# Two pieces of work change places on the tensor engine in the dilated attention scores

## The chip, the cores and the metric

One core of one Trainium2 chip runs the whole program. The metric is the device time of one execution in microseconds (us), the median of three. The engines are named as in the profile: PE is the tensor engine (PEld its weight loads, which overlap), DVE the vector engine, ACT the scalar engine, POOL GpSimd, SP the engine that issues most of the transfers. They run side by side, each through its own program in order, and wait for one another by semaphores: a number that one instruction raises when it is done, and that another waits for.

## The reference, cut to what matters

The program is a stack of layers over 512 tokens: two hybrid layers (delta rule and gated linear attention), then a stick-breaking attention, a feed-forward block, a dilated attention and another feed-forward block. The change is in the dilated attention alone, where the softmax of windowed scores is computed for three groups of eight heads each:

```python
DIL_GROUPS = ((128, 1), (512, 4), (2048, 16))
DIL_HEADS = 8
DIL_HEAD_DIM = 64
...
    s = jnp.einsum('brhnqd,brhnkd->brhnqk', q_blk, k_blk).astype(jnp.float32) * (dh ** -0.5)
    s = jnp.where(mask[None, None, None], s + bias[None, None, :, None], NEG)
    lse = jax.nn.logsumexp(s, axis=-1)
    p = jnp.exp(s - lse[..., None])
    o = jnp.einsum('brhnqk,brhnkd->brhnqd', p.astype(v_blk.dtype), v_blk)
```

All of it is in float32.

## The kernel before

`dilated_scores` does this in 15 **units**. A unit is a group g, a tile t of 128 query tokens, and either all eight heads against one tile of 128 keys (unit 0, and units 7 to 14, which are groups 1 and 2), or four heads against two tiles of keys (units 1 to 6, group 0). Either way a unit has 128 x 1024 scores. Its stages are:

- PE, `scores(n)` (line 2292): the products of queries and keys, with a contraction of 64 rows. They go to two of the four score banks in PSUM; even and odd units have two each.
- DVE, `bias(n)` (line 2343 twice, then 2346): adds the bias table while it copies the scores out to the SBUF tile `scores`, and takes the negated maximum of every row.
- ACT, `exps(n)` (line 2370): the exponentials in place, one instruction for each head, which also gives the row's sum.
- PE, `turn(n)` (line 2301): eight 128 x 128 transposes of the weights into PSUM banks 4 and 5.
- DVE, `turned(n)` (line 2354, twice): copies the turned weights to the SBUF tile `weights_turned`.
- PE, `values(n)` (line 2316): sixteen weight loads and matmul records (eight products of 64 columns), turned weights by values, into PSUM bank 6 or 7.
- ACT, `copy_out(n)` (line 2376): copies a finished tile of 512 columns to `numerators`, once for each of the 12 tiles.

`scores`, `weights_turned` and the score banks are double-buffered, by the parity of the unit. Banks 4 and 5 are not: `turn(n)` waits until the copies of unit n-1 are done. `scores(n)` waits until `bias(n-2)` is done, and `bias(n)` until unit n-2 is turned.

The order on each engine is written out by hand in one loop for each engine (the PE loop stands behind `values`, the DVE loop behind `turned`). PE runs `scores(n)`, `turn(n-1)`, `values(n-2)` for rising n; DVE `bias(n)`, `turned(n-1)`; ACT `exps(n)`, `copy_out(n-3)`. `dilated_merge` follows, whose first work on PE is at line 2405 and on ACT at line 2437; it begins when the stage's own work is done.

Of the kernel before, what the change touches and what calls it, by code (L numbers as in the profile page):

```python
# [127 lines left out]
def sbuf(nc, name, shape, dtype):  # L128
    NAMES[name] += 1
    return nc.sbuf_tensor(f"{name}_{NAMES[name]}", shape, dtype)  # L130


@contextmanager
def phase(nc, *names, landed=()):


    stack = ExitStack()
    NAMES["phase"] += 1
    sems = {n: stack.enter_context(nc.semaphore(f"{n}_{NAMES['phase']}")) for n in names}
    for s in USED:  # L140
        nc.sync.sem_clear(s)
    for held in HELD:
        held.close()
    yield named(**sems)
    HELD[:] = [stack]
    USED[:] = [*sems.values(), *landed]
# [2111 lines left out]
def dilated_scores(nc, k, q, kk, v, tables, num, top, total):  # L2258

    ps, con = k.ps, k.con
    ident = con[:, K_IDENT:K_IDENT + P]

    units = [(0, 0, 0, 8, 1)] + [(0, t, h0, 4, 2) for t in range(1, TT) for h0 in (0, 4)] \
        + [(g, t, 0, 8, 1) for g in (1, 2) for t in range(TT)]
    n_units = len(units)
    tiles = [n for n, (g, t, h0, heads, _) in enumerate(units) if h0 + heads == DIL_HEADS]
    with ExitStack() as stack, phase(nc, "scores", "half", "biased", "exp", "turned", "turned_read", "out", "out_copy") as s:  # L2270
        sc = stack.enter_context(sbuf(nc, "scores", [P, 2, 2 * T], F32))
        pt = stack.enter_context(sbuf(nc, "weights_turned", [P, 2, 8, P], F32))

        def exps(n):
            return sum(u[3] for u in units[:n])

        def tile_of(n):
            return sum(1 for m in tiles if m < n)

        with nc.Block() as block:  # L2280
            @block.tensor
            def _(pe):
                def scores(n):
                    g, t, h0, heads, keys = units[n]
                    b = 2 * (n % 2)
                    if n >= 2:
                        pe.wait_ge(s.biased, n - 1)
                    for hd in range(h0, h0 + heads):
                        rows = slice(64 * (hd % 2), 64 * (hd % 2) + 64)
                        at = (hd - h0) // 2 * keys * P  # L2290
                        f = 4 * g + hd // 2
                        mm = pe.matmul(ps[:, b + hd % 2, at:at + keys * P], q[rows, f, t * P:(t + 1) * P],
                                       kk[rows, f, (t + 1 - keys) * P:(t + 1) * P], start=True, stop=True)
                    mm.then_inc(s.scores, 1)

                def turn(n):
                    pe.wait_ge(s.exp, exps(n + 1))
                    if n >= 1:
                        pe.wait_ge(s.turned_read, 2 * n)
                    for m in range(8):  # L2300
                        mm = pe.transpose(ps[:, 4 + m // 4, m % 4 * P:(m % 4 + 1) * P],
                                          sc[:, n % 2, m * P:(m + 1) * P], ident)
                        if m % 4 == 3:
                            mm.then_inc(s.turned, 1)

                def values(n):
                    g, t, h0, heads, keys = units[n]
                    out = 6 + tile_of(n) % 2
                    pe.wait_ge(s.turned_read, 2 * n + 2)
                    if tile_of(n) >= 2:  # L2310
                        pe.wait_ge(s.out_copy, tile_of(n) - 1)
                    for hd in range(h0, h0 + heads):
                        for kt in range(keys):

                            m = (hd % 2) * 4 + (hd - h0) // 2 * keys + kt
                            mm = pe.matmul(ps[:, out, hd * 64:hd * 64 + 64], pt[:, n % 2, m],
                                           v[:, t + 1 - keys + kt, g, hd * 64:hd * 64 + 64],
                                           start=kt == 0, stop=kt == keys - 1)
                    mm.then_inc(s.out, 1)
                for n in range(n_units + 2):  # L2320
                    if n < n_units:
                        scores(n)
                    if 1 <= n <= n_units:
                        turn(n - 1)
                    if n >= 2:
                        values(n - 2)

            @block.vector
            def _(dve):
                def bias(n):  # L2330
                    g, t, h0, heads, keys = units[n]
                    b = 2 * (n % 2)
                    w = keys * P
                    hh = heads // 2
                    tab = tables[g][:, h0:h0 + heads, :]
                    if g == 0 and keys == 1:
                        tab = tab[:, :, P:]
                    dst = sc[:, n % 2].rearrange("p (y h w) -> p y h w", y=2, h=hh)
                    dve.wait_ge(s.scores, n + 1)
                    if n >= 2:  # L2340
                        dve.wait_ge(s.turned, 2 * (n - 1))
                    for y in range(2):
                        dve.tensor_tensor(dst[:, y], ps[:, b + y].rearrange("p (h w) -> p h w", h=hh),
                                          tab.rearrange("p (h y) w -> p y h w", y=2)[:, y], ALU.add).then_inc(s.half, 1)
                    dve.wait_ge(s.half, 2 * n + 2)
                    dve.tensor_reduce(top[:, TT * g + t, h0:h0 + heads].rearrange("p (h y) -> p y h", y=2), dst, AX_X,
                                      ALU.max, negate=True).then_inc(s.biased, 1)

                def turned(n):
                    for half in range(2):  # L2350
                        dve.wait_ge(s.turned, 2 * n + half + 1)
                        if n >= 2:
                            dve.wait_ge(s.out, n - 1)
                        dve.tensor_copy(pt[:, n % 2, 4 * half:4 * half + 4],
                                        ps[:, 4 + half].rearrange("p (m i) -> p m i", m=4)).then_inc(s.turned_read, 1)
                for n in range(n_units + 1):
                    if n < n_units:
                        bias(n)
                    if n >= 1:
                        turned(n - 1)  # L2360

            @block.scalar
            def _(act):
                def exps(n):
                    g, t, h0, heads, keys = units[n]
                    act.wait_ge(s.biased, n + 1)
                    for hd in range(h0, h0 + heads):
                        at = hd % 2 * T + (hd - h0) // 2 * keys * P
                        x = sc[:, n % 2, at:at + keys * P]
                        act.activation(x, x, ACT.Exp, bias=top[:, TT * g + t, hd:hd + 1],  # L2370
                                       accum_out=total[:, TT * g + t, hd:hd + 1]).then_inc(s.exp, 1)

                def copy_out(n):
                    g, t = units[n][0:2]
                    act.wait_ge(s.out, n + 1)
                    act.copy(num[:, TT * g + t], ps[:, 6 + tile_of(n) % 2]).then_inc(s.out_copy, 1)
                for n in range(n_units + 3):
                    if n < n_units:
                        exps(n)
                    if n - 3 in tiles:  # L2380
                        copy_out(n - 3)
# [275 lines left out]
```

## Time and profile before

| | us |
|---|---|
| median of 3 runs | 2292.49 |
| the three runs | 2287.30, 2292.49, 2296.38 |
| the profiled execution | 2290.96 |
| its span, first to last instruction | 2289.20 |
| PE busy | 2077.6 (91%) |
| DVE busy | 1181.4 (52%) |
| ACT busy | 870.1 (38%) |
| POOL busy | 342.5 (15%) |
| the stage of `dilated_scores` (1746.0 to 1827.3) | 81.3 |

The span is what the page and the trace divide up; the device time of the same execution is 1.76 us longer. The three runs lie within 9.1 us. Most of the program is large matrix products in which PE is the bound. The stage that is changed is 3.6% of the span. Shares of the whole program say little about it, so it is read from its own stretch of the trace.

### The profile page before, as it was taken

Reading aid. Unit: us, or ns where it says so; the run is one execution under the profiler, and the core shown is the slowest. Engines: PE = TensorE matmul, PEld = TensorE weight load, DVE = VectorE, ACT = ScalarE, POOL = GpSimd, SP = SyncE. Lnnn points to the kernel's source line nnn. Section 1 sums busy time; section 2 is a strip of 40 time slices with the busy share of each in tenths; the row PEclk is TensorE's granted clock in tenths of the full one; section 3 lists DMA queues with packets and bytes.
Section 4 is the critical chain, followed back from the end, with each engine's and each line's share of the span. In section 5 each row is a group of like instructions: output and inputs, shape, how many; then the busy total and the mean of one; then the engine's idle time right before and its main releaser. Section 6 shows DMA issues by size and latency. Waiting matters only on the chain. (4 is left out here: it accounts for less than half of the span.)

```text
span 2289.2 us, 28407 instructions
## 1 busy us (share of the span) xinstructions
PE 2077.6 (91%) x11540; PEld 1630.2 (71%) x11540; DVE 1181.4 (52%) x1435; ACT 870.1 (38%) x1249; POOL 342.5 (15%) x322
## 2 busy tenths in 40 slices
PE   8999888799988889887999999989997859999996
PEld 4777866477786668643778888868895746888885
DVE  4445653444565353243487457454324657854753
ACT  4236432533644241354344234332122625432431
POOL 1200632120063220133110000120000032000002
PEclk9999999899999999999999999999999889999998
DMA  5221011222101122100222322222221012223221
GB/s 207 74 74 56 3 74 37 94 73 74 56 3 74 37 92 92 37 1 1 83 83 87 105 94 105 88 74 102 101 92 37 1 37 74 92 89 105 105 82 62
DMA packets 27167, 163.65 MB, mean 71 GB/s; under 512 B 2755, under 2 KB 6267, under 8 KB 11420
## 3 DMA queue, kind: packets, MB, share of 16 engines
q1 hardware_dynamic: 27036, 161.81, 19.9%
q8 instruction: 93, 1.52, 0.3%
q14 instruction: 38, 0.31, 0.0%
HBM read 155.47 MB, written 6.33 MB: 71 GB/s over the span
## 5 line engine op out<-in xcount | busy, mean ns | idle before, releaser
L251 PE MATMUL psum<-inputs_high,weights_high 128*128 128x512 f32 x928 | 376.7, 406 | 15.6 <-DVE inputs_low L232 8.7
L253 PE MATMUL psum<-inputs_high,weights_low 128*128 128x512 f32 x928 | 362.0, 390 | 0.0
L252 PE MATMUL psum<-inputs_low,weights_high 128*128 128x512 f32 x928 | 361.7, 390 | 0.0
L1843 PE MATMUL psum<-inputs_high,weights_high 128*128 128x512 f32 x704 | 276.4, 393 | 7.9 <-DVE inputs_low L1981 7.9
L237 DVE TENSOR_TENSOR weights_low<-weights_raw,weights_high 128x2048 fp32r<-128x2048 f32 x72 | 168.6, 2342 | 209.2 <-ACT weights_high L226 209.1
L1844 PE MATMUL psum<-inputs_low,weights_high 128*128 128x512 f32 x704 | 274.7, 390 | 0.0
L1845 PE MATMUL psum<-inputs_high,weights_low 128*128 128x512 f32 x704 | 274.4, 390 | 0.0
L226 ACT CAST weights_high<-weights_raw 128x2048 fp32r<-128x2048 f32 x72 | 136.7, 1899 | 230.8 <-PE psum L253 191.5
L251 PEld LDWEIGHTS psum<-inputs_high,weights_high 128*128 128x128 f32 x928 | 174.1, 188 | 70.4 <-DVE inputs_low L232 13.5
L252 PEld LDWEIGHTS psum<-inputs_low,weights_high 128*128 128x128 f32 x928 | 174.3, 188 | 37.8 <-issue 4.3
L253 PEld LDWEIGHTS psum<-inputs_high,weights_low 128*128 128x128 f32 x928 | 174.2, 188 | 37.2
L1828 ACT CAST weights_high<-weights_raw 128x2048 fp32r<-128x2048 f32 (+1 forms) x76 | 127.0, 1671 | 161.5 <-PE psum L1845 160.9
L1835 DVE TENSOR_TENSOR weights_low<-weights_raw,weights_high 128x2048 fp32r<-128x2048 f32 (+1 forms) x76 | 152.5, 2007 | 37.2 <-ACT weights_high L1828 37.2
L1843 PEld LDWEIGHTS psum<-inputs_high,weights_high 128*128 128x128 f32 x704 | 132.4, 188 | 40.5 <-DVE inputs_low L1981 12.8
L1845 PEld LDWEIGHTS psum<-inputs_high,weights_low 128*128 128x128 f32 x704 | 132.6, 188 | 27.9
L1844 PEld LDWEIGHTS psum<-inputs_low,weights_high 128*128 128x128 f32 x704 | 132.5, 188 | 27.6 <-issue 0.5
L2007 DVE SCALAR_TENSOR_TENSOR conv<-up_scaled,second_parameters,conv 128x511 f32<-128x511 f32 (+1 forms) x176 | 131.8, 749 | 21.6 <-ACT conv L1933 18.5
L1843 PE MATMUL psum<-hidden_high,weights_high 128*128 128x512 f32 x352 | 137.4, 390 | 0.5
L1844 PE MATMUL psum<-hidden_low,weights_high 128*128 128x512 f32 x352 | 137.0, 389 | 0.0
L1845 PE MATMUL psum<-hidden_high,weights_low 128*128 128x512 f32 x352 | 136.9, 389 | 0.0
L2000 DVE TENSOR_TENSOR up_scaled<-psum,inverse_rms 128x512 f32<-128x512 f32 x88 | 60.7, 689 | 94.1 <-PE psum L1845 90.0
L1933 ACT ACTIVATE conv<-up_scaled,second_parameters 128x512 f32<-128x512 f32 x88 | 71.9, 817 | 92.8 <-DVE up_scaled L2000 92.8
(334 smaller groups left out, 3335.9 us busy)
## 6 DMA issues: line engine op xcount, KB each, us to landing
weights_raw<-w_stream SPq DMA_DIRECT2D x116, 1024.0 KB, 4.8
weights_raw<-w_down SPq DMA_DIRECT2D x32, 704.0 KB, 4.1
residual_parked<-residual SPq DMA_DIRECT2D x2, 2048.0 KB, 10.0
residual_back<-residual_parked SPq DMA_DIRECT2D x2, 2048.0 KB, 7.8
residual<-x_t SPq DMA_DIRECT2D x1, 2048.0 KB, 7.7
out_t<-residual SPq DMA_DIRECT2D x8, 256.0 KB, 2.0
constants<-consts SPq DMA_DIRECT2D x1, 1537.5 KB, 11.5
table_backward<-bias_rows SPq DMA_DIRECT2D x1, 1024.0 KB, 5.7
```

The costliest lines, as they stand in the source:

```text
L226: act.copy(self.whi[:, u, 0:self.cols], self.raw[:, u, 0:self.cols]).then_inc(s.high, 1)
L237: dve.tensor_tensor(self.wlo[:, u, 0:self.cols], self.raw[:, u, 0:self.cols], self.whi[:, u, 0:self.cols].bitcast(F32), ALU.subtract).then ...
L251: pe.matmul(out, hi, self.ahi[:, k], start=start and b == 0, stop=False)
L252: pe.matmul(out, hi, self.alo[:, k], start=False, stop=False)
L253: mm = pe.matmul(out, lo, self.ahi[:, k], start=False, stop=stop and b == blocks - 1)
L1828: act.copy(whi[:, c % 2, 0:cols], raw[:, c % 2, 0:cols]).then_inc(s.high, 1)
L1835: dve.tensor_tensor(wlo[:, c % 2, 0:cols], raw[:, c % 2, 0:cols], whi[:, c % 2, 0:cols].bitcast(F32), ALU.subtract).then_inc(s.split, 1)
L1843: pe.matmul(out, wh, hi, start=start, stop=False)
L1844: pe.matmul(out, wh, lo, start=False, stop=False)
L1845: return pe.matmul(out, wl, hi, start=False, stop=stop)
L1933: act.activation(y[:, n % 2, yy], up[:, n % 2, yy], ACT.Identity, scale=taps[:, layer, 2, yy, n:n + 1], bias=bias[:, layer, yy, n:n + 1]). ...
L2007: dve.scalar_tensor_tensor(y[:, n % 2, yy, back:], up[:, n % 2, yy, 0:T - back], taps[:, layer, 2 - back, yy, n:n + 1], y[:, n % 2, yy, ba ...
```

## The change

In the PE loop, `scores(n+2)` now comes right behind `turn(n)`, and `values(n-1)` behind that; before, `values(n-1)` came between the two. The first two scores stand ahead of the loop. The DVE loop is written in another form. No instruction is added or taken away, and no wait is.

```diff
-                for n in range(n_units + 2):
+                scores(0)
+                scores(1)
+                for n in range(n_units + 1):
                     if n < n_units:
-                        scores(n)
-                    if 1 <= n <= n_units:
-                        turn(n - 1)
-                    if n >= 2:
-                        values(n - 2)
+                        turn(n)
+                    if n + 2 < n_units:
+                        scores(n + 2)
+                    if n >= 1:
+                        values(n - 1)
...
-                for n in range(n_units + 1):
-                    if n < n_units:
-                        bias(n)
-                    if n >= 1:
-                        turned(n - 1)
+                bias(0)
+                bias(1)
+                for n in range(n_units):
+                    turned(n)
+                    if n + 2 < n_units:
+                        bias(n + 2)
```

On PE, in the middle of the stage where units of eight heads follow one another, this is the order before (L2292 scores, L2301 the transposes of the turn, L2316 values):

```order
L2301 MATMUL psum<-constants,scores 128x128 x8
L2316 MATMUL psum<-dilated_v,weights_turned 128x64 x8
L2292 MATMUL psum<-dilated_k,dilated_q 128x128 x8
L2301 MATMUL psum<-constants,scores 128x128 x8
L2316 MATMUL psum<-dilated_v,weights_turned 128x64 x8
```

And this is the order with the change at the same place (the lines carry the same numbers):

```order
L2301 MATMUL psum<-constants,scores 128x128 x8
L2292 MATMUL psum<-dilated_k,dilated_q 128x128 x8
L2316 MATMUL psum<-dilated_v,weights_turned 128x64 x8
L2301 MATMUL psum<-constants,scores 128x128 x8
L2292 MATMUL psum<-dilated_k,dilated_q 128x128 x8
```

The scores have moved ahead of the values, from unit 3 to unit 14; behind the last scores, the order is the same in both kernels.

On DVE, from the start of the stage, this is the order before (L2343 bias, L2346 the maximum, L2354 the copy of turned weights):

```order
L2343 TENSOR_TENSOR scores<-psum,bias 128x512 x2
L2346 TENSOR_REDUCE negative_maxima<-scores 128x2x4
L2343 TENSOR_TENSOR scores<-psum,bias 128x512 x2
L2346 TENSOR_REDUCE negative_maxima<-scores 128x2x2
L2354 COPY weights_turned<-psum 128x512 x2
L2343 TENSOR_TENSOR scores<-psum,bias 128x512 x2
```

And this with the change, where the line numbers are two higher:

```order
L2345 TENSOR_TENSOR scores<-psum,bias 128x512 x2
L2348 TENSOR_REDUCE negative_maxima<-scores 128x2x4
L2345 TENSOR_TENSOR scores<-psum,bias 128x512 x2
L2348 TENSOR_REDUCE negative_maxima<-scores 128x2x2
L2356 COPY weights_turned<-psum 128x512 x2
L2345 TENSOR_TENSOR scores<-psum,bias 128x512 x2
```

Nothing has moved there. `bias(0)`, `bias(1)`, `turned(0)`, `bias(2)`, `turned(1)` and so on is what both loops give, down to the end.

## Rows read from the trace of the kernel before

**Rows 1.** The page's head: the span.
```profile
span 2289.2 us, 28407 instructions
```

**Rows 2.** Windows: stretch, length, busy time (x instructions) by engine, granted clock, DMA, GB/s.
```profile
core 0: us, PE busy (x) PEld busy (x) DVE busy (x) ACT busy (x) POOL busy (x), PEclk, DMA share, GB/s
1756.40:1817.80 61.40, 49.90 (x476) 45.48 (x472) 48.12 (x65) 39.53 (x177) 0.00 (x0) 1.00 0.00 1
1817.80:1831.40 13.60, 12.54 (x59) 10.85 (x60) 1.38 (x2) 4.45 (x9) 0.00 (x0) 0.50 0.01 2
1831.40:1834.80 3.40, 0.83 (x7) 0.42 (x5) 0.68 (x1) 2.67 (x3) 0.00 (x0) 0.99 0.00 0
```

**Rows 3.** Waits, 1744 to 1830: who waited for whom, total us, times, longest.
```profile
ACT scores L2370 <- DVE negative_maxima L2346: 44.2, 14, 20.9
...
PE psum L2301 <- ACT scores L2370: 16.6, 12, 5.0
DVE scores L2343 <- PE psum L2292: 12.8, 11, 1.5
```

**Rows 4.** Timeline, two units of eight heads: start, length, engine, line, [idle before].
```profile
1790.32 0.40 ACT L2370 ACTIVATE scores<-scores,negative_maxima 128x128 f32<-128x128 f32 x1 [1.78 <-DVE negative_maxima L2346]
...
1793.41 0.56 ACT L2376 COPY numerators<-psum 128x512 f32<-128x512 f32 x1
...
1793.56 1.09 PE L2301 MATMUL psum<-constants,scores 128*128 128x128 f32 x8 [1.05 <-ACT scores L2370]
...
1794.49 1.90 PE L2316 MATMUL psum<-dilated_v,weights_turned 128*128 128x64 f32 x16
...
1796.31 1.16 PE L2292 MATMUL psum<-dilated_k,dilated_q 64*128 64x128 f32 x16
...
1797.52 1.29 DVE L2343 TENSOR_TENSOR scores<-psum,bias 128x512 f32<-128x512 f32 x2 [1.23 <-PE psum L2292]
...
1798.84 1.22 DVE L2346 TENSOR_REDUCE negative_maxima<-scores 128x8 f32<-128x1024 f32 x1
...
1800.10 0.40 ACT L2370 ACTIVATE scores<-scores,negative_maxima 128x128 f32<-128x128 f32 x1 [1.31 <-DVE negative_maxima L2346]
```

**Rows 5.** Timeline, DVE and PE among the units of four heads.
```profile
1767.92 1.28 DVE L2354 COPY weights_turned<-psum 128x512 f32<-128x512 f32 x2
...
1770.17 1.09 PE L2301 MATMUL psum<-constants,scores 128*128 128x128 f32 x8 [0.93 <-ACT scores L2370]
...
1771.10 1.90 PE L2316 MATMUL psum<-dilated_v,weights_turned 128*128 128x64 f32 x16
1771.74 1.28 DVE L2354 COPY weights_turned<-psum 128x512 f32<-128x512 f32 x2
...
1772.92 1.14 PE L2292 MATMUL psum<-dilated_k,dilated_q 64*128 64x256 f32 x8
1773.99 1.09 PE L2301 MATMUL psum<-constants,scores 128*128 128x128 f32 x8
```

**Rows 6.** Timeline, PE: other turns, units 0, 2, 3, 7 and 8 by their starts.
```profile
1753.06 1.97 PE L2301 MATMUL psum<-constants,scores 128*128 128x128 f32 x8 [4.99 <-ACT scores L2370]
...
1754.96 1.81 PE L2292 MATMUL psum<-dilated_k,dilated_q 64*128 64x256 f32 x8
...
1761.53 1.09 PE L2301 MATMUL psum<-constants,scores 128*128 128x128 f32 x8 [0.93 <-ACT scores L2370]
...
1765.35 1.09 PE L2301 MATMUL psum<-constants,scores 128*128 128x128 f32 x8
...
1783.78 1.09 PE L2301 MATMUL psum<-constants,scores 128*128 128x128 f32 x8 [1.04 <-ACT scores L2370]
...
1788.59 1.09 PE L2301 MATMUL psum<-constants,scores 128*128 128x128 f32 x8 [0.90 <-ACT scores L2370]
```

**Rows 7.** Timeline, the stage's end and the first steps of the merge.
```profile
1813.12 1.09 PE L2301 MATMUL psum<-constants,scores 128*128 128x128 f32 x8 [1.05 <-ACT scores L2370]
...
1817.93 1.97 PE L2301 MATMUL psum<-constants,scores 128*128 128x128 f32 x8 [1.99 <-ACT scores L2370]
...
1819.70 6.92 PE L2316 MATMUL psum<-dilated_v,weights_turned 128*128 128x64 f32 x32
...
1826.66 0.58 ACT L2376 COPY numerators<-psum 128x512 f32<-128x512 f32 x1 [2.83 <-PE psum L2316]
1827.55 1.01 PE L2405 MATMUL psum<-constants,negative_maxima 128*8 128x128 f32 x4 [0.93 <-PEq L2280]
...
1829.45 0.57 ACT L2437 COPY top_and_total<-psum 8x512 f32<-8x512 f32 x1 [0.28 <-PE psum L2405]
```

## The prediction

> **What bounds the kernel now.** The whole span is 2289.2 us [rows 1], and the change touches one stage of it, `dilated_scores`, so I read that stage alone, in three steps. First the windows [rows 2]: between 1756.4 and 1817.8 PE is busy for 49.90 of 61.40 us, DVE for 48.12 and ACT for 39.53, at a full granted clock, with no transfers to speak of. None of the three is busy all the time, so either the limit changes from place to place or it is a chain that runs through all of them. Then the waits [rows 3]: ACT waits for the maxima of DVE, PE's turn waits for ACT's exponentials (16.6 us, 12 times), and DVE's bias waits for PE's scores (12.8 us, 11 times). Each engine waits for the next in a ring, so it is a chain. Third the timeline of two units of eight heads [rows 4], which gives the ring by its starts: exponentials 1790.32, turn 1793.56, values 1794.49, scores 1796.31, bias 1797.52, maximum 1798.84, next exponentials 1800.10. The exponentials that start at 1800.10 belong to the unit two further on than those of 1790.32: the other parity runs in between. So one round of 9.78 us makes two units, 4.89 each.
>
> The steps of the round, from the starts in [rows 4]: exponentials to turn 3.24, turn to values 0.93, values to scores 1.82, scores to bias 1.21, bias to maximum 1.32, maximum to exponentials 1.26; the sum is 9.78. The values are in the round only because they stand ahead of the scores in PE's queue. Nothing in the ring needs their result.
>
> **The change part by part.**
>
> *DVE.* The two loops give one and the same order of instructions, so what the new form says of copying first is worth nothing. Its 0 us needs no cover.
>
> *PE, units of eight heads.* The scores of unit n+2 go ahead of the values of unit n-1. Their own wait is for the bias of unit n, which ended before unit n's exponentials and so before its turn: nothing new to wait for. The copies that the values need ended before the turn of unit n could start. So the swap takes 1.82 us out of the round, plus or minus what the first scores cost behind a transpose instead of behind values. The trace shows that switch once, at the half clock: turn 1753.06, scores 1754.96, 1.90 apart, when the turn itself lasts 1.97 [rows 6]. So the scores start right behind, and at the full clock I take 0.93, as from turn to values [rows 4]. The round is then 9.78 - 1.82 = 7.96 us, 3.98 a unit.
>
> What is late next? PE's own queue: turn to values 0.93, values to scores 1.82, scores to turn 1.07 (1772.92 to 1773.99, where the turn waited for nothing [rows 5]), in all 3.82. DVE: from one pair of copies to the next where nothing was waited for, 1767.92 to 1771.74, is also 3.82 [rows 5]. ACT: from the start of the exponentials to the end of the copy out, 1793.41 + 0.56 - 1790.32 = 3.65 [rows 4]. All three are below 3.98, DVE and PE by 0.16 only. The chain stays the bound, but barely.
>
> *PE, units of four heads.* Their exponentials are shorter. From turn 1761.53 to turn 1770.17 [rows 5, 6] is 8.64 for two units, 4.32 each; without 1.82 the round would be 6.82, or 3.41 each, below the floor of 3.82. So there it is PE and DVE that bound, at 3.82.
>
> *The sum, turn by turn.* Units 0 to 3 keep their times: the third turn starts at 1761.53 because of exponentials that began before any moved scores matter, and the fourth, at 1765.35, is already 3.82 behind it [rows 6]. From there: turn 4 at 1769.17 (before 1770.17), turn 5 at 1772.99, turn 6 at 1776.81. Turn 7 is the first behind eight-head exponentials, and DVE decides it: the copies of unit 3, at 1767.92 before [rows 5], are 1.0 earlier, 1766.92, those of unit 5 two steps of 3.82 on, 1774.56; then 1.37 to the bias of unit 7 (3.82 less the 1.32 and the 1.13 from maximum to copies), 1.32, 1.26 and 3.24 give 1781.75, where it was 1783.78 [rows 6], 2.0 earlier. Turn 8 follows at the floor: 1785.57, 3.03 earlier than 1788.59. From turn 8 to turn 14 are three rounds, before 1817.93 - 1788.59 = 29.34 [rows 6, 7], now 3 x 7.96 = 23.88. The last turn starts at 1809.45, **8.5 us earlier**.
>
> *The tail.* The last turn takes 1.97 us and the 32 records of the last two values 6.92, and all that is at a granted clock of 0.50 [rows 2, 7]: the lower level, 1.2 GHz. The drop came at 1817.8, behind 1.99 us in which PE had nothing to do [rows 7]. Waits of 0.90 to 1.05 before each turn, at the same place in the cycle, did not bring it [rows 4, 6, 7]. In the changed kernel the last turn comes about 3.9 us behind the one before it, of which turn and values take 0.93 + 1.90 = 2.8, so PE idles for about 1.1 us, near the harmless ones. At the full clock the tail costs 0.92 for the turn, 1.83 + 1.90 for the values and 0.6 for the copy out, 5.3 us from the turn's start, where it was 1826.66 + 0.58 - 1817.93 = 9.31 [rows 7]. That is **4.0 us** if the clock holds, 0 if it does not.
>
> *Behind the stage.* The merge starts at the lower clock, too; ACT's copies there wait 0.28 us each time for four transposes, and longer for the first four, which take 1.01 [rows 7]. At the upper clock these halve: 0.5 for the first and 0.3 for each of the next two, about **1.0 us**. It falls away with the clock. Further on the merge is a chain of small steps and nothing in it moves. Transfers are not waited for.
>
> Sum: 8.5 + 4.0 + 1.0 = 13.5 us off the profiled execution's 2290.96, so 2277.4. The median of the runs shown is 1.5 us above the profiled one; the forecast of a median is **2279.0 us**, 0.6% less.
>
> *A rule against a row.* After 1831.4 the granted clock is 0.99 again [rows 2], and what PE did from 1827.55 until then was transposes alone (line 2405 [rows 7]): here transposes bring the upper level back. The Trainium skill, in TensorE: Matmul & The Clock Gate, Part 4 (PE-mode transpose), says the upper level doesn't engage for transposes. By that rule the last turn would not help to hold the clock, and the tail would fall to the lower level as before, which is the first rival's time. The trace speaks against it.
>
> **The rivals.**
>
> *The clock falls in the tail all the same.* For it: 1.1 us of idle is a little over anything seen without a drop here, and the last values are the thinnest work of the stage. Against it: every wait of about 1 us is followed by a full clock. Then only 8.5 us are won: 2292.5 - 8.5 = **2284.0 us**. The same holds in part if the drop comes later, among the values.
>
> *The switch has a price on PE.* If scores behind transposes, or values behind scores, start 0.5 us later than their neighbours show, PE's floor is 4.3 instead of 3.82. Then the units of four heads win nothing, those of eight 0.6 each over seven, some 4 us: **2288 us**. The only row of the switch shows no such price [rows 6].
>
> *Slower.* The same mechanism with a larger price: PE's queue becomes the ring. From 4.89 - 3.82 = 1.07 us a unit on it costs time; at 1.5 us a unit it would be 7 x 0.43 + 5 x 1.0 = 8 us more, **2300 us**. It would need moved scores that hold back the values, and these the next turn.
>
> *It does nothing.* If another wait closes the ring, such as the bias for the copies ahead of it in DVE's queue: copies start behind the maximum and last 1.28. With turns 3.98 apart they end just before the scores are there, by 0.1 us, so this can cost tenths a unit, not the gain. **2292 us** only if I have read the waits wrongly.
>
> **How the numbers follow.** Forecast case 0.64, clock falls 0.20, a price on the switch 0.08, nothing 0.04, slower 0.04. The range: single runs lie up to 5 us from their median, so 2279 reaches down to 2274; upward it takes in the fallen clock at 2284 and about half of what lies beyond, to 2288. A change of 0.5%, 11.5 us, is about what can be told from none, and the forecast of 13.5 is just over it; so the forecast case gives faster by more than that in three of four (0.48), the fallen clock in one of five (0.04). Faster 0.52, same 0.44, slower 0.04.
>
> **What would show it.** The stage's timeline with scores directly behind each turn; two units of eight heads in about 7.96 us; DVE's wait for scores down from 1.1 to 1.2 us to a tenth or two; no wait for ACT before the turns of four-head units; the last turn near 1809.4; a granted clock of 1.00 through the tail, and last values of about 3.8 us. It is wrong if the turns stand over 4.2 us apart, if any record of lines 2292 to 2316 has grown longer than before at the same clock, or if the last copy out ends later than 1819.

## The result and the profile after

The changed kernel takes 2280.59 us in the median of seven runs (2278.91 to 2284.68), the kernel before 2292.49 (seven runs, 2287.30 to 2296.38). The ratio is 0.995, with a 95% interval of 0.9937 to 0.9963: 12 us, or 0.5%, less, and the interval keeps clear of 1.

The profiled execution of the changed kernel is the slowest of its seven, 2284.68 us with a span of 2283.0, so the spans of the two profiles ([rows 1] and this one) differ by 6.2 us only. The stage tells more. First its windows in the changed kernel, with the columns of [rows 2]: from behind the second turn to just ahead of the last one, and the tail.

```profile
1763.70:1815.00 51.30, 49.95 (x468) 44.65 (x466) 47.18 (x64) 39.61 (x177) 0.00 (x0) 1.00 0.00 1
1815.00:1820.40 5.40, 4.61 (x40) 4.47 (x40) 1.29 (x2) 2.15 (x5) 0.00 (x0) 1.00 0.01 3
```

PE is busy for 49.95 of 51.30 us, where before it was 49.90 of 61.40 [rows 2], a window that holds the eight records of one turn more: nearly the same work, with the gaps gone. The tail, at a granted clock of 0.50 before, is at 1.00. The waits of the changed kernel in 1744 to 1826, to be read against [rows 3]:

```profile
ACT scores L2373 <- DVE negative_maxima L2348: 37.5, 14, 22.7
...
PE psum L2301 <- ACT scores L2373: 6.3, 3, 5.0
...
DVE scores L2345 <- PE psum L2292: 4.4, 10, 1.5
```

PE waits ahead of a turn three times instead of twelve (one of the three is the first turn, one the last), and DVE's wait for the scores has shrunk from 12.8 to 4.4 us. And this is the timeline of one round, among units of eight heads, against [rows 4]:

```profile
1787.03 1.09 PE L2301 MATMUL psum<-constants,scores 128*128 128x128 f32 x8
...
1788.05 1.16 PE L2292 MATMUL psum<-dilated_k,dilated_q 64*128 64x128 f32 x16
1789.15 2.00 PE L2316 MATMUL psum<-dilated_v,weights_turned 128*128 128x64 f32 x16
1789.26 1.29 DVE L2345 TENSOR_TENSOR scores<-psum,bias 128x512 f32<-128x512 f32 x2 [0.25 <-PE psum L2292]
1790.59 1.22 DVE L2348 TENSOR_REDUCE negative_maxima<-scores 128x8 f32<-128x1024 f32 x1
1790.98 1.04 PE L2301 MATMUL psum<-constants,scores 128*128 128x128 f32 x8
...
1791.84 0.40 ACT L2373 ACTIVATE scores<-scores,negative_maxima 128x128 f32<-128x128 f32 x1 [0.96 <-DVE negative_maxima L2348]
...
1795.08 1.09 PE L2301 MATMUL psum<-constants,scores 128*128 128x128 f32 x8
```

The steps by their starts: turn to scores 1.02, scores to bias 1.21, bias to maximum 1.33, maximum to exponentials 1.25, exponentials to turn 3.24. That is 8.05 us for two units, where it was 9.78, and the values (1789.15) now lie beside the bias instead of ahead of it. Their sixteen records take 2.00 us instead of 1.90 [rows 4]. The longest record of line 2316 in the whole changed kernel takes 0.323 us, and 0.276 us in the kernel before with its clock held (the first experiment below). The stage's end, against [rows 7]:

```profile
1815.08 1.09 PE L2301 MATMUL psum<-constants,scores 128*128 128x128 f32 x8 [1.08 <-ACT scores L2373]
...
1816.01 3.68 PE L2316 MATMUL psum<-dilated_v,weights_turned 128*128 128x64 f32 x32
...
1819.73 0.59 ACT L2379 COPY numerators<-psum 128x512 f32<-128x512 f32 x1 [1.20 <-PE psum L2316]
1820.62 0.60 PE L2408 MATMUL psum<-constants,negative_maxima 128*8 128x128 f32 x4 [0.93 <-PEq L2280]
```

Since the two profiles begin the stage at different times (the first turn at 1753.06 before, 1758.63 after), everything is compared by differences within it:

| us | predicted | before | after |
|---|---|---|---|
| first turn to last turn | 64.87 to 56.39 | 64.87 | 56.45 |
| round of two eight-head units | 7.96 | 9.78 | 8.05 |
| a unit of four heads | 3.82 | 4.32 | 3.88 |
| last turn to end of last copy out | 5.3 | 9.31 | 5.24 |
| from there to the merge's first work on DVE | 1.0 less | 6.86 | 5.68 |

In sum 13.7 us are gone from this stretch of the changed kernel's profile; 13.5 were forecast. The span shows 6.2, because 5.6 us were lost ahead of the stage's first turn and about 1.9 behind the merge's first work on DVE, in code that the change doesn't touch. Of the 5.6, 3.9 were lost before line 2073, which builds the bias tables, had begun (1740.36 against 1736.47), and 1.7 in its sixteen matmuls: they took 10.21 us at a mean granted clock of 0.68, where it was 8.53 us and 0.83 in the profile of before. The 5.6 belong to this one execution: in the nine other profiles of this document the first turn starts between 1751.81 and 1755.16. Of the 1.9, 1.7 lie in the last 21 us of the program, where the matmuls of lines 1453 and 1454 took 2.04 and 1.82 us instead of 1.10 and 1.02. The section on the clock in the tail comes back to this.

### The profile page after: what moved, and what is told of

It reads as the page before. It is cut to its first block and busy times, and to the rows that moved or that the text cites. A ratio compares the mean times of both kernels' runs of the same rounds, so it can differ in the third digit from the quotient of the medians.

```text
span 2283.0 us, 28407 instructions
## 1 busy us (share of the span) xinstructions
PE 2076.0 (91%) x11540; PEld 1627.0 (71%) x11540; DVE 1180.0 (52%) x1435; ACT 869.6 (38%) x1249; POOL 343.2 (15%) x322
```

## The experiments

All times below are medians; each group of runs had its own runs of the kernel before on the same chip (2292.66 us for the first four, 2291.01 us for the others).

### Is the slow tail the clock's doing?

The kernel before, with work in the gap ahead of the last turn:

```diff
+                def filler(count, bank):
+                    for m in range(count):
+                        pe.transpose(ps[:, bank, m % 4 * P:(m % 4 + 1) * P], con[:, K_IDENT:K_IDENT + P], ident)
...
                     if n >= 2:
                         values(n - 2)
+                    if n == n_units - 1:
+                        pe.wait_ge(s.biased, n_units - 1)
+                        filler(12, 3)
```

> The kernel before, with one addition: behind the values of unit 12, in the 1.99 us in which PE idles ahead of the last turn, twelve transposes of the identity into a score bank that nobody reads any more. Theory (the tail was slow because the granted clock fell behind the idle time): the clock stays at 1.00 through the tail, the last turn takes 1.1 instead of 1.97 us, the 32 records of the last values 3.7 instead of 6.92, from the start of the last turn to the end of the last copy out 5.3 instead of 9.31 us, and the merge is 1 us shorter: 5 us less than before, about 2287.5, ratio 0.998. The round of two units stays 9.78 us. Rival (the last values are slow by themselves, having nothing to alternate with): the tail stays at about 9.3 us, the time at 2292.5 or a little more.

Measured: 2288.53 us, ratio 0.9981 (0.9972 to 0.9990), 4.1 us less. Its window over the last turn and the tail, with the columns of [rows 2]:

```profile
1816.70:1822.00 5.30, 4.61 (x40) 4.47 (x40) 1.29 (x2) 2.11 (x4) 0.00 (x0) 1.00 0.00 0
```

The clock is at 1.00, the last turn (1816.75) takes 1.09 us, and from it to the end of the last copy out (1821.39 + 0.58) are 5.22 us, as in the changed kernel (5.24). The first and the last turn are 64.94 apart, where it was 64.87. So the tail's 4 us are the clock's and don't need the new order of scores and values; twelve useless transposes win them as well. The rival, values that are slow by themselves, is out.

### Do the values stand in the round before, and not after?

The same edit in both kernels: half the values. Both kernels then leave out the second head of every pair, so their results are wrong; they serve to measure the stage alone.

```diff
-                    for hd in range(h0, h0 + heads):
+                    for hd in range(h0, h0 + heads, 2):
...
-                            m = (hd % 2) * 4 + (hd - h0) // 2 * keys + kt
-                            mm = pe.matmul(ps[:, out, hd * 64:hd * 64 + 64], pt[:, n % 2, m],
-                                           v[:, t + 1 - keys + kt, g, hd * 64:hd * 64 + 64],
+                            m = (hd - h0) // 2 * keys + kt
+                            mm = pe.matmul(ps[:, out, hd * 64:hd * 64 + 128], pt[:, n % 2, m],
+                                           v[:, t + 1 - keys + kt, g, hd * 64:hd * 64 + 128],
```

> The kernel before with half the values: each pair of heads uses the turned weights of the first of them in one product of 128 columns, so that four weight loads and products replace eight; the second head's output is left out. Theory (before, the values stand in the round): from turn to turn plus two, among units of eight heads, the round falls by the time the values lose, from 9.78 to about 8.9 us if they take 0.93; among units of four heads from 8.64 to about 7.8. From the first to the last turn 64.9 falls to about 59.5. Rival (the round is set by ACT and DVE, and the values lie beside them): the round stays at 9.7 or more and the last turn comes less than 1 us earlier.

Measured: 2284.27 us, ratio 0.9963 (0.9950 to 0.9975). In the round of two eight-head units of this kernel, values and scores are now 0.99 apart instead of 1.82:

```profile
1788.24 1.09 PE L2301 MATMUL psum<-constants,scores 128*128 128x128 f32 x8 [1.08 <-ACT scores L2370]
...
1789.17 1.06 PE L2316 MATMUL psum<-dilated_v,weights_turned 128*128 128x128 f32 x8
...
1790.16 1.16 PE L2292 MATMUL psum<-dilated_k,dilated_q 64*128 64x128 f32 x16
```

The turns stand at 1788.24 and 1797.18, a round of 8.94 instead of 9.78; first to last turn is 59.91. Of 0.83 us less of values, 0.84 arrives in the round: the values stood in it at full price.

> The changed kernel with the same half of the values left out. Theory (values no longer in the round of eight-head units, but PE's queue bounds the units of four heads): the round of eight-head units stays at 8.05 us, within 0.1, and the units of four heads go from 3.88 to about 3.65 each, where DVE takes over; from the first to the last turn 56.4 falls by about 1 us only. In the tail PE idles for about 2 us again, as in the kernel before, so the granted clock may fall there; if it does, the last turn takes 1.97 us. Rival (PE's queue bounds all of it now): the eight-head round falls too, to 7.5 us or less.

Measured: 2274.57 us, ratio 0.9927 (0.9913 to 0.9940). The turns of eight-head units stand at 1780.10, 1788.15 and 1796.20: 8.05 a round, unmoved by the halved values. In the units of four heads they stand at 1764.41, 1768.06, 1771.70 and 1775.35: 3.65 a unit instead of 3.88. PE now waits ahead of each of these turns:

```profile
1768.06 1.09 PE L2301 MATMUL psum<-constants,scores 128*128 128x128 f32 x8 [0.40 <-ACT scores L2373]
...
1780.10 1.09 PE L2301 MATMUL psum<-constants,scores 128*128 128x128 f32 x8 [1.48 <-ACT scores L2373]
...
1788.15 1.09 PE L2301 MATMUL psum<-constants,scores 128*128 128x128 f32 x8 [1.13 <-ACT scores L2373]
```

First to last turn is 55.62, 0.8 less. The same edit is worth 5.0 us between the first and the last turn of the kernel before and 0.8 in the changed one. That settles the mechanism: the change took the values out of the chain, and PE's queue bounds the four-head units alone. The medians are a coarser measure here. This one is 6.0 us below the changed kernel's; the 0.8 of the stage and what the two profiles show from the last turn to the end of the program (465.0 against 467.9 us) make 3.7, and the rest is open. Its six runs fall into two groups, 2273.7 to 2274.6 and 2279.4 to 2279.5. The clock did not fall in either tail here, though PE idled for 2.17 us ahead of the last turn of the kernel before with half values; that went against the prediction's reading of the clock, and led to the last section of experiments.

### Scores in front of the turn

```diff
-                    if n < n_units:
-                        turn(n)
                     if n + 2 < n_units:
                         scores(n + 2)
+                    if n < n_units:
+                        turn(n)
```

> The changed kernel with scores of unit n+2 one step further ahead, in front of the turn of unit n; values behind the turn. The scores then lie in PE's wait for the exponentials, and the bias of unit n+2 waits for the turn of unit n, because it overwrites what the turn reads. Theory (the chain of eight-head units is exponentials, turn, scores, bias, maximum): without the scores it is 3.24 + 1.2 + 1.32 + 1.26 = 7.0 us a round, below PE's floor of 3.88 a unit, so turns stand 3.9 apart instead of 4.02; from the first to the last turn about 55 instead of 56.4 us: 1.3 us less than the changed kernel, about 2279.5, not to be told from it by the time. Rival (PE waits for something else, and a turn that comes 1 us later behind the scores costs the chain as much as before): 56.4 or more.

Measured: 2278.40 us, ratio 0.994 (0.9922 to 0.9958); by its interval not to be told from the change. The stage, however, is clearer than expected: first to last turn is 53.68, 2.8 less than with the change, not 1.4. Two turns and what is between them in this kernel:

```profile
1788.59 1.09 PE L2301 MATMUL psum<-constants,scores 128*128 128x128 f32 x8
...
1789.52 1.90 PE L2316 MATMUL psum<-dilated_v,weights_turned 128*128 128x64 f32 x16
...
1791.34 1.16 PE L2292 MATMUL psum<-dilated_k,dilated_q 64*128 64x128 f32 x16
```

The next turn is at 1792.44, right behind these scores: every turn from the third on stands 3.82 to 3.86 behind the one before, in units of four and of eight heads alike. PE's waits for the exponentials between 1760 and 1806 are down to one:

```profile
PE psum L2301 <- ACT scores L2373: 1.0, 1, 1.0
```

That one is the last turn but one, which has no scores ahead of it any more. Up to there, with the scores off the chain, PE is simply full: turn to values 0.93, values to scores 1.82, scores to turn 1.10. My 55 us allowed for a longer step at the first eight-head unit and for 3.9 us a unit; the step is 3.85 us here (4.10 in the changed kernel) and the others are 3.82 to 3.86, and that is the 1.3 us by which I missed.

### The start of the stage

In every profile up to here the first turn took 1.93 to 1.97 us, at the lower clock, behind 4.99 us of idle [rows 6]; with scores in front of the turn the idle time was 1.77 and 2.09 us, with those scores in between. Now PE is kept at work there. The edit is shown against the kernel with scores in front of the turn, and `filler` is that of the first experiment:

```diff
                 scores(0)
                 scores(1)
+                filler(14, 7)
                 for n in range(n_units + 1):
                     if n + 2 < n_units:
                         scores(n + 2)
+                    if n == 0:
+                        filler(18, 7)
                     if n < n_units:
                         turn(n)
```

> Scores in front of the turn, as in the run before, and PE kept at work at the start of the stage: fourteen transposes of the identity behind the scores of unit 1 and eighteen behind those of unit 2, into a bank that the values fill later. In every trace so far PE stands nearly idle for 5 us there and the granted clock is 0.50 when the first turn begins. Theory: with the clock held, the first turn takes 1.1 instead of 1.97 us and turn 1 follows sooner than 3.70 us behind; from the first to the last turn 53.7 falls by 0.8 to 1.6 us. Together about 2277, 0.6 to 0.7% below the kernel before, the best of all so far by a hair. Rival (the exponentials of unit 1 decide when turn 1 starts, the clock is covered): 53.7 stays.

Measured: 2273.44 us, ratio 0.9926 (0.9912 to 0.9939), the lowest median of a kernel with a right result, 17.6 us below the kernel before. Its interval overlaps that of the version without the filler, so it is the stage that tells the two apart. The granted clock is 1.00 from before the first turn to the last:

```profile
1748.00:1753.40 5.40, 5.31 (x45) 4.20 (x42) 4.55 (x6) 3.20 (x17) 0.00 (x0) 1.00 0.00 0
1753.40:1806.30 52.90, 50.21 (x481) 46.34 (x480) 48.93 (x67) 41.62 (x185) 0.00 (x0) 1.00 0.01 1
```

The first turn takes 1.09 us, turn 1 follows 2.13 behind instead of 3.70, and first to last turn is 52.89, 0.8 less than without the filler, at the low end of what I expected: of the 1.57 us of head start, 0.64 go again at turn 2, which waits for the exponentials of unit 2 (turn 1 to turn 2 is 4.46 instead of 3.82), and 0.14 at turn 7.

### How often does the clock fall in the tail of the kernel before?

> The kernel before, unchanged, in a second profiled execution. In the first, the granted clock fell 0.1 us ahead of the last turn, behind 1.99 us of idle; but the kernel before with half the values idled 2.17 us at the same place and kept its clock. If the drop belongs to the idle time, it comes again here, the last turn takes 1.97 us and the way from it to the end of the last copy out 9.3 us. If it depends on something that changes from execution to execution, it may fall at another place or not at all: then 5.3 us, and up to 5 us of the difference between the two kernels are not in every execution.

> The kernel before, unchanged, in a third profiled execution, for the same question: how often the last turn and the last values run at the lower clock. The drop in all three would make the 5 us of the tail and the merge a fixed part of the gain; one or two of three would make it a part that differs from execution to execution.

> The kernel before, with forty transposes of the identity behind the scores of unit 1, so that PE works until the first turn. Theory (the half clock at the first turn comes from the idle time ahead of it): the first turn takes 1.1 us and turn 1 follows less than 3.64 us behind it. The rest of the stage keeps its round of 9.78 us; its tail is a fourth look at whether the clock falls at the end.

The edit of the last one, with the same `filler`:

```diff
                     if n < n_units:
                         scores(n)
+                    if n == 1:
+                        filler(40, 7)
```

Measured, single runs: 2290.33, 2290.59 and 2289.91 us. The clock fell in the tail of all three, but not alike. The second execution of the kernel before, window by window and with the end of its tail:

```profile
1817.90:1821.40 3.50, 3.49 (x17) 3.50 (x18) 1.38 (x2) 0.90 (x2) 0.00 (x0) 0.51 0.02 5
1821.40:1831.40 10.00, 5.54 (x49) 4.64 (x48) 0.91 (x2) 5.88 (x8) 0.00 (x0) 1.00 0.00 1
...
1819.66 4.50 PE L2316 MATMUL psum<-dilated_v,weights_turned 128*128 128x64 f32 x32
```

It came back among the last values, which took 4.50 us instead of 6.92. In the third execution it stayed low to the end, as in the first:

```profile
1817.60:1831.20 13.60, 12.67 (x59) 10.89 (x60) 1.38 (x2) 4.44 (x8) 0.00 (x0) 0.50 0.01 2
```

With the filler at the start of the stage it fell later, behind the last turn, which took 1.09 us:

```profile
1818.37 1.09 PE L2301 MATMUL psum<-constants,scores 128*128 128x128 f32 x8 [1.98 <-ACT scores L2375]
...
1819.30 6.35 PE L2316 MATMUL psum<-dilated_v,weights_turned 128*128 128x64 f32 x32
```

| kernel | last turn to last copy out | from there to the merge on DVE | from there to the end of the span |
|---|---|---|---|
| before, first profile | 9.31 | 6.86 | 455.1 |
| before, second | 6.87 | 5.68 | 458.1 |
| before, third | 9.31 | 6.86 | 455.2 |
| before, filler at the start | 7.90 | 6.86 | 455.1 |
| before, filler in the tail | 5.22 | 5.69 | 456.0 |
| changed | 5.24 | 5.68 | 457.0 |
| scores in front of the turn | 5.24 | 5.68 | 455.7 |
| the same with filler at the start | 5.24 | 5.68 | 455.2 |

In the tail and the merge's start the kernel before loses 5.3, 1.6 and 5.3 us against a held clock in its three executions, 4.0 in the mean. But the last column moves too. The second execution, which lost least in the tail, took 3.0 us more behind it; part of that is the first products of the feed-forward block, which ran at the lower clock there. The same instruction in the first profile and in the second:

```profile
1869.55 0.39 PE L252 MATMUL psum<-inputs_low,weights_high 128*128 128x512 f32 x1
...
1866.39 0.63 PE L252 MATMUL psum<-inputs_low,weights_high 128*128 128x512 f32 x1
```

Counted from the last turn to the end of the span, the three executions are alike: 471.3, 470.7 and 471.3 us. The four kernels whose clock held through the tail (the last four of the table) take 466.2 to 467.9, 4.2 less in the mean. That is what the held tail is worth to the whole program by the profiles, and the filler in the tail gave 4.1 by the medians. From the first to the last turn are 64.96 and 64.94 us in the second and third execution, 64.87 in the first: the chain repeats to 0.1 us from execution to execution, while the clock does not. The filler at the start brought 1.6 us there (63.31), as the first turn took 1.09 us and turn 1 followed 2.12 behind instead of 3.64.

## Why the prediction was right

*The chain.* The ring of six steps read from [rows 4] was the bound of the eight-head units, and the values stood in it only by their place in the queue. Halving them in either kernel shows it directly: 0.84 us a round before, nothing after. The saving between the first and the last turn was forecast at 8.5 us and is 8.42. That it agrees to a tenth is partly luck. Counted from the first turn against the forecast, turn 3 came 0.36 us late (of which 0.27 had gone by turn 1 to a lower clock that lasted longer: turn 1 took 1.61 us instead of 1.09), turn 6 0.55 late, turn 7 0.29 early, turn 8 0.16 early, and the three rounds behind it took 24.10 instead of 23.88; errors of up to 0.8 us of either sign cancelled.

*The price of the switch.* I took 0.93 us from a turn to the scores behind it, as from turn to values; it is 1.02 (0.98 where the turn itself started right behind values), and from scores to values 1.1. This is the second rival's mechanism, with a price of a tenth instead of half a microsecond: the round is 8.05 instead of 7.96. The prediction also named a longer record in lines 2292 to 2316 at the same clock as a sign of being wrong. Taken by its letter the sign came, in the values (0.323 against 0.276 us); it was drawn too tight, for the same tenth.

*The floors.* PE's was put at 3.82 a unit and is 3.88, for the same reason. DVE's I also put at 3.82, by the copies at 1767.92 and 1771.74 [rows 5], between which I said that nothing was waited for. That reading was wrong: with half the values taken out of the changed kernel, the four-head units run at 3.65 a unit, so that DVE's work fits there. In the kernel before, the bias started 1.37 us behind the start of its copies, and the scores that it needs had ended only 0.04 us ahead of it:

```profile
1768.11 1.14 PE L2292 MATMUL psum<-dilated_k,dilated_q 64*128 64x256 f32 x8
...
1769.29 1.29 DVE L2343 TENSOR_TENSOR scores<-psum,bias 128x512 f32<-128x512 f32 x2
```

In the changed kernel it starts 1.20 behind them (copies 1768.76, bias 1769.96). That is why turn 7 came 28.40 us behind the first turn and not the forecast 28.69, although the turns ahead of it were late. Among the four-head units nothing came of it, as PE has the higher floor, but the sentence that both stand 0.16 below the chain held for PE alone.

*The tail.* Held clock, 4.07 us less in the tail and 1.2 in the merge, where 4.0 and 1.0 were forecast. The clock held in the one profile of the changed kernel, and in those of the two versions built on it. What the prediction put at nothing is the rest of the program: it said that further on nothing moves. The clock's falls there do differ from execution to execution, and together with them the held tail is worth 4.2 us in the mean rather than 5.0 (3.2 by the changed kernel's own profile). The expected gain is then 8.4 + 4.2 = 12.6 rather than 13.5 us. Measured by the medians: 11.9. So this term was over-sized by about 0.9 of the 1.6 us that lie between 2279.0 and 2280.59; the other 0.7 can't be told from the spread of the runs (the seven of the kernel before span 9 us).

*The clock and its idle times.* I argued that 1.1 us of idle is harmless and 1.99 is not. The first held (1.08 us ahead of the last turn). The second is looser than I put it: behind 1.98 and 1.99 us of idle the clock fell at once in the kernel before, 1.5 us later in the one with a filler at its start, and behind 2.17 us, in the kernel with half values, not at all. The length of the one gap ahead of a turn is then not what decides by itself.

*Transposes and the clock.* In [rows 2, 7] the upper level came back during transposes alone. The fillers show that transposes also hold it: at the start of the kernel before, forty of them fill all but 0.48 us of PE's gap, and the clock is 1.00 from ahead of them until it falls in the tail:

```profile
1741.40:1819.90 78.50, 65.37 (x579) 56.65 (x578) 60.01 (x82) 45.72 (x202) 0.00 (x0) 1.00 0.00 1
```

The twelve of the tail kept it, too. The Trainium skill, in TensorE: Matmul & The Clock Gate, Part 4 (PE-mode transpose), says that the upper level doesn't engage for transposes. These runs don't agree, for float32 transposes at least: 1.00 through both fillers, and 0.99 behind the merge's transposes [rows 2].

*The DVE loop.* Its order is the same in both kernels, and no row of DVE in the changed kernel comes in another order than before. It was right to cost it at nothing.

## What to carry to other kernels

When several engines wait for one another in turn, write down one round from the starts in the timeline and ask of each step whether the next one needs its result; work that is in the ring only by its place in a queue goes behind what the ring waits for. Then compare the new round with every engine's own sum, and take those sums from stretches where really nothing was waited for, small gaps included. Where PE thins out at the end or the start of a stage, look at the granted clock: a dozen transposes of no use gave 4.1 us here, where the whole change, which holds the clock in the same place, gave 11.9. But count such a gain to the end of the program and over several executions, not in one stretch of one profile.

## What the runs showed of the hardware

How long the granted clock stays low behind a gap differs from execution to execution in the same kernel: behind the same 1.98 to 1.99 us of idle the last values took 4.50 us in one profile and 6.92 in another (and 6.35, with the drop coming later, in the kernel with forty transposes at its start). What one stretch gains can go again in another: the execution that lost 3.6 us less in the tail took 3.0 us more behind it. A half clock through work that keeps PE busy can last: in two executions of the kernel before it stayed at 0.50 for 13.6 us, with PE busy for 12.5 and more of them, mostly on weight loads of 128 x 128 with products of 64 columns. And scores with a contraction of 64 rows start up to 0.1 us later behind a transpose than values do (0.98 to 1.02 against 0.93 us after the turn's start).
